# Forty tokens instead of thirty-two on fetched expert rows, the low parts of value units in pairs

## The chip, the cores and the metric

The kernel runs on 1 core of one Trainium2 chip. The time is device microseconds (us) of one execution. The engines are TensorE (PE), VectorE (DVE), ScalarE (ACT), GpSimd (POOL) and SyncE (SP, which only issues transfers here).

## The reference

One layer on 256 tokens of 1024 channels: a mixer (attention and a recurrence), then a feed-forward part that picks, for each token and each of 8 heads, 16 of 16384 experts. An expert is one row of `peer_u` and one row of `peer_v`, 1024 float32 each. The change lies in the feed-forward part.

```python
def peer_ffn(xn, peer_wq, peer_subkeys, peer_u, peer_v):
    q = (xt @ peer_wq).reshape(n_tok, PEER_HEADS, 2, PEER_HALF)        # 256 tokens, 8 heads, 2 x 128
    s = jnp.einsum('thpc,hpnc->thpn', q, peer_subkeys)                 # 128 subkeys for each half
    top_s, top_i = lax.top_k(s, PEER_TOPK)                             # 16 of 128
    cand_s = (top_s[:, :, 0, :, None] + top_s[:, :, 1, None, :])       # 16 x 16 candidates
    cand_i = (top_i[:, :, 0, :, None] * PEER_NKEYS + top_i[:, :, 1, None, :])
    best_s, best_pos = lax.top_k(cand_s, PEER_TOPK)                    # 16 experts of 16384 per head
    idx = jnp.take_along_axis(cand_i, best_pos, axis=-1)
    gates = jax.nn.softmax(best_s, axis=-1)
    def one_chunk(args):
        u_g = peer_u[ic]
        h = jax.nn.gelu(jnp.einsum('chkd,cd->chk', u_g, xc)) * gc      # dot with row of u, gelu, gate
        v_g = peer_v[ic]
        return jnp.einsum('chk,chkd->cd', h, v_g)                      # weighted sum of rows of v

def reference(x, ...):
    xn = rmsnorm(h, norm1_g[l])
    h = h + hybrid_mixer(xn, ...)                                      # attention and a recurrent mixer
    xn = rmsnorm(h, norm2_g[l])
    h = h + peer_ffn(xn, peer_wq[l], peer_subkeys[l], peer_u[l], peer_v[l])
    return rmsnorm(h, normf_g)
```

## The kernel before, in words

**Two ways to compute an expert.** The experts are a grid of 128 x 128. For the first 224 tokens (TD) the kernel computes all 16384 experts densely, in 128 units of 128 experts, and makes the gates of the experts that were not picked zero. For the last 32 tokens (TG) it fetches only the rows that were picked. A token has 8 x 16 = 128 picks. The 128 partitions are 32 tokens times 4 repeats (REPS), so one indirect transfer on GpSimd's queue fetches 128 rows of 4 KB, one for each partition, and 32 of them (GATHERS) cover the u rows, 32 more the v rows. A row that was fetched costs VectorE one operation over 128 x 1024: `dot` (product with the repeated token and sum) for u, `row_added` (sum += coefficient x row) for v.

**A unit.** float32 products are made from high and low parts rounded to TensorE's one-pass type. A u unit (`expert_unit`) is 8 matmuls of the unit's high part with both parts of 224 tokens, 448 columns (L922), and 8 of its low part with the high part of the tokens, 224 columns (L926). A v unit is the same (`wide_value` L988, `low_value` L993). SyncE loads the unit (512 KB) into one of 4 slots (`load`, L396) once the unit four before it is done, ScalarE makes the high part `hi` (L1069), GpSimd the low part `lo` over the raw data (L1509); in the v stage VectorE makes it (L2176).

**The order in the u stage.** 128 units, numbered 0 to 127 here. Beside the first 52, VectorE ranks the picks. From unit 68 (FIRST) the units are gated: after unit n's 16 matmuls, TensorE makes the gates of 4 tokens from one-hot rows with 8 short matmuls (L948, L949; the "hot group"). There are SECOND = 56 of these groups, for 224 tokens, so the last 4 units have none. The hot group of unit n waits for `oh1_low`, which ScalarE makes in `low_one_hots` (L1398) from what VectorE made in `one_hots` (L2092, L2094). ScalarE works strictly in order: in step n it makes `hi` of unit n+2, copies the right half of unit n (L1414), makes gelu of unit n-1 (L1419) and then the low one-hots of unit n+1. VectorE's step n is gates in (L2104), halves (L2111), `gated` of n-1 (L2119) and the one-hots of unit n+2.

**SyncE's queue** is one program in order. After the load of unit 79 it issues 3 transfers that repeat the last 32 tokens over the partitions (L442) and 4 that lay out the picks and gates in the same way (L446), SBUF to SBUF, and then goes on with the load of unit 80.

**GpSimd's queue**: the low parts of all u units; behind each of the last four one fetch; two low parts of v units; then the rest of the fetches, each as soon as one of 4 row buffers is free. VectorE does one `dot` or `row_added` behind every second v unit.

**The end.** The last two v units are interleaved over the 8 output blocks, and one more matmul per block (L1056, float32, two instructions) adds the 32 fetched tokens' sums. Then the output is turned, normalised and stored.

## Time and profile before

| | |
|---|---|
| runs | 987.2, 987.57, 988.05 us, median 987.57 us |
| profiled execution | 987.29 us, its span in the profile 985.5 us |
| granted TensorE clock, mean | 0.998 of full |
| busy | PE 975.0 us (99%), DVE 743.3 (75%), ACT 626.6 (64%), POOL 598.1 (61%) |
| u stage, v stage | from 296 us to 651 us, from 651 us to 977 us |
| transfers | 215.05 MB, mean 218 GB/s; by slice of 24.6 us in the v stage some 315, at most 383 GB/s |

Columns of the views are named where their rows stand. A matmul's own duration overlaps the next ones; how far matmuls are apart is read from the chain of waits, where eight in a row take, for instance, 1.64 us. A time in square brackets is idle time of the engine before the instruction, with what ended it.

### The profile page before, as it was taken

The numbers are of one execution on the slowest core, as the hardware profiler recorded it, in microseconds if no ns is written. First come the engines' busy times: TensorE is split into PE (matmuls) and PEld (weight loads), VectorE is DVE, ScalarE is ACT, GpSimd is POOL, SyncE is SP. The second block draws the span as 40 slices with busy tenths as digits, with TensorE's granted clock in tenths as the row PEclk, the third lists the DMA queues.
The fourth block names the chain that finished last, engine by engine and source line by source line (L and its number), as shares of the span: only waits on it lengthen the run. The fifth ranks groups of instructions, "written<-read, shape, count | busy, mean of one in ns | idle before, by whom it ended". The sixth has DMA issues, their size and how long they took to land.

```text
span 985.5 us, 22607 instructions
## 1 busy us (share of the span) xinstructions
PE 975.0 (99%) x7344; PEld 918.3 (93%) x7344; DVE 743.3 (75%) x1718; ACT 626.6 (64%) x1232; POOL 598.1 (61%) x292
## 2 busy tenths in 40 slices
PE   9999999999999999999999999999999999999997
PEld 8998899999899999999999999989999999999996
DVE  7664663544747797887788888879888878888886
ACT  6774375556556666676988888865555555555553
POOL 3685624687318999989777777874443335444420
PEclk9999999999999999999999999999999999999999
DMA  7463303355545555555554444499888887988871
GB/s 264 141 238 121 128 35 107 129 188 195 204 162 171 210 203 208 211 201 209 188 189 170 170 170 170 171 355 383 311 317 316 317 309 280 333 317 313 305 276 44
DMA packets 61821, 215.05 MB, mean 218 GB/s; under 512 B 7203, under 2 KB 9251, under 8 KB 61644
## 3 DMA queue, kind: packets, MB, share of 16 engines
q1 hardware_dynamic: 51980, 180.04, 51.0%
q0 software_dynamic: 9216, 33.56, 9.4%
q10 hardware_dynamic: 576, 0.82, 0.2%
q8 instruction: 29, 0.48, 0.2%
q14 instruction: 20, 0.16, 0.1%
HBM read 212.89 MB, written 1.06 MB: 217 GB/s over the span
## 4 chain that ended last, share of the span: by engine, by line
PE 96%; POOL 2%; DVE 1%; ACT 1%; DMA 0%; issue 0%; ACTq 0%; DVEq 0%; POOLq 0%
PE PS L988 21%; PE PS L922 21%; PE PS L993 12%; PE PS L926 11%; PE PS L493 4%; PE PS L494 4%; PE PS L495 4%; PE PS L871 3%; PE PS L503 2%; PE PS L879 2%; PE PS L948 1%; POOL lo L1509 1%; PE PS L949 1%; PE PS L657 1%; PE PS L507 1%; PE PS L912 1%
## 5 line engine op out<-in xcount | busy, mean ns | idle before, releaser
L1509 POOL TENSOR_TENSOR lo<-raw,hi 128x1024 fp32r<-128x1024 f32 x191 | 459.4, 2413 | 152.7 <-ACT hi L1069 139.2
L922 PE MATMUL PS<-xb,hi 128*128 128x448 f32 x1024 | 235.0, 371 | 0.0
L1069 ACT CAST hi<-raw 128x1024 fp32r<-128x1024 f32 x203 | 212.7, 1048 | 33.2 <-DMA raw<-in_u_units 12.4
L988 PE MATMUL PS<-xb,hi 128*128 128x448 f32 x1008 | 228.7, 368 | 0.0
L922 PEld LDWEIGHTS PS<-xb,hi 128*128 128x128 f32 x1024 | 183.0, 189 | 12.2
L988 PEld LDWEIGHTS PS<-xb,hi 128*128 128x128 f32 x1008 | 179.9, 189 | 11.8
L2176 DVE TENSOR_TENSOR lo<-raw,hi 128x1024 fp32r<-128x1024 f32 x126 | 154.1, 1223 | 24.2 <-ACT hi L1406 24.1
L1443 ACT CAST xb<-arena 128x224 fp32r (+1 forms) x126 | 47.9, 380 | 143.6 <-PE PS L993 142.3
L926 PEld LDWEIGHTS PS<-xb,lo 128*128 128x128 f32 x1024 | 133.8, 191 | 4.7 <-POOL lo L1509 0.7
L993 PEld LDWEIGHTS PS<-xb,lo 128*128 128x128 f32 x1008 | 132.7, 191 | 4.1
L1406 ACT CAST hi<-raw 128x1024 fp32r<-128x1024 f32 x128 | 133.9, 1046 | 3.4 <-DMA raw<-in_v_units 3.4
L926 PE MATMUL PS<-xb,lo 128*128 128x224 f32 x1024 | 133.9, 273 | 0.4 <-POOL lo L1509 0.4
L993 PE MATMUL PS<-xb,lo 128*128 128x224 f32 x1008 | 132.8, 273 | 0.0
L1549 POOL DMA_INDIRECT arena<-in_v_units,con x32 | 66.5, 2079 | 95.0 <-DVE hot L2170 70.9
L1549 POOL DMA_INDIRECT arena<-in_u_rows,con x32 | 59.5, 1859 | 79.0 <-DVE arena L2163 78.4
L493 PE MATMUL PS<-xb,hi 128*128 128x256 f32 x264 | 76.0, 288 | 0.1
L494 PE MATMUL PS<-xb,hi 128*128 128x256 f32 x264 | 74.7, 283 | 0.0
L495 PE MATMUL PS<-xb,lo 128*128 128x256 f32 x264 | 74.7, 283 | 0.0
L1398 ACT ACTIVATE oh_low<-oh_high,gt 128x128 f16<-128x128 f16 x224 | 70.8, 389 | 0.1
L2157 DVE TENSOR_TENSOR xb<-arena,xb 128x224 fp32r<-128x224 f32 x126 | 52.0, 413 | 18.5 <-ACT xb L1443 18.3
L2092 DVE TENSOR_SCALAR oh_high<-PS,i2T,gT 128x128 f16<-128x128 f16 x224 | 61.2, 336 | 0.1
L2104 DVE SCALAR_TENSOR_TENSOR arena<-PS,arena 128x512 f32 (+1 forms) x56 | 38.8, 692 | 24.5 <-PE PS L949 24.3
(353 smaller groups left out, 1517.0 us busy)
## 6 DMA issues: line engine op xcount, KB each, us to landing
raw<-in_u_units SPq DMA_DIRECT2D x128, 512.0 KB
raw<-in_v_units SPq DMA_DIRECT2D x128, 512.0 KB
raw<-in_w_in_units SPq DMA_DIRECT2D x43, 512.0 KB
raw<-in_w_q_units SPq DMA_DIRECT2D x16, 512.0 KB
raw<-in_w_proj_units SPq DMA_DIRECT2D x8, 512.0 KB
raw<-in_w_out_units SPq DMA_DIRECT2D x8, 512.0 KB
arena<-bias_rows SPq DMA_DIRECT2D x2, 512.0 KB, 5.0
arena<-in_subkeys_t SPq DMA_DIRECT2D x1, 1024.0 KB, 5.4
```

The lines of the kernel that those rows point to most:

```text
L493: mm(ps, hi[:, s, c], mh[:, k, :], start=(k == k0), stop=False)
L494: mm(ps, hi[:, s, c], ml[:, k, :], start=False, stop=False)
L495: last = mm(ps, lo[:, s, c], mh[:, k, :], start=False, stop=(k == k1 - 1))
L922: mm(o[:, 0:2 * TD].rearrange("p (s t) -> p s t", s=2), hi[:, w, P * k:P * k + P], xb[:, k, :, 0:TD], start=(k == 0), stop=False, skip_gro ...
L926: last = mm(o[:, 0:TD], lo[:, w, P * k:P * k + P], xb[:, k, 0, 0:TD], start=False, stop=(k == KT - 1), skip_group_check=True)
L988: return mm(PS[:, V_BANKS[c], 0:2 * TD].rearrange("p (s t) -> p s t", s=2), hi[:, (U_V + j) % 4, P * c:P * c + P], coef_slot(u + j)[:, :, ...
L993: return mm(PS[:, V_BANKS[c], 0:TD], value_slot(j)[:, P * c:P * c + P], coef_slot(u + j)[:, 0, 0:TD], start=False, stop=last, skip_group_c ...
L1069: nc.scalar.copy(hi[:, j, :], raw[:, j, :]).then_inc(hi_made, 1)
L1406: nc.scalar.copy(hi[:, (U_V + j) % 4, :], value_raw(j % 8)).then_inc(hi_made, 1)
L1509: nc.gpsimd.tensor_tensor(lo[:, w, :], raw[:, w, :], hi[:, w, :].bitcast(F32), ALU.subtract).then_inc(lo_pool, 1)
L1549: nc.gpsimd.indirect_dma_start(out=rows_at[g % 4], out_offset=None, in_=rows, in_offset=bass.IndirectOffsetOnAxis(ap=pick_row[:, n:n + 1], ...
L2176: V.tensor_tensor(value_slot(j), value_raw(j), hi[:, (U_V + j) % 4, :].bitcast(F32), ALU.subtract).then_inc(lo_dve, 1)
```

## The change

Tokens on fetched rows go from 32 to 40, as two groups: 32 tokens x 4 repeats as before, and the last 8 tokens x 16 repeats, with 8 fetches of u rows and 8 of v rows. TD is 216, so the dense matmuls have 432 and 216 columns. SECOND is 54, so 6 units at the end of the u stage have no hot group. In all there are 80 fetches and 80 row operations.

- SyncE repeats the 8 tokens with 15 more transfers and lays out their picks with 16 more, all at the same place in its queue.
- GpSimd fetches the first 8 (the u rows of the second group) behind the low parts of units 84, 88, ... 112, and VectorE makes their dots in the gated steps of units 88, 92, ... 116, ahead of the one-hots of that step. The loops there are written out.
- The other 72 row operations are spread evenly over the v stage, in the order of the list ROW_WORK.
- VectorE makes `gl` and `lo` of value units two at a time: one operation over 2 x 216 and one over 2 x 1024 columns.
- ScalarE copies the repeated rows of both groups (4 copies for 2) and makes gelu of the first dots apart.
- One more matmul per output block adds the second group.

```diff
-TG = 32
+GROUPS = [32, 8]
+TG = sum(GROUPS)
 TD = T - TG
 SECOND = TD // 4
-FIRST = NKEYS - SECOND - 4
+FIRST = 68
 GATED_UNITS = NKEYS - FIRST
-REPS = P // TG
-GATHERS = P // REPS
+REPEATS = [P // tokens for tokens in GROUPS]
+GATHERS = sum(GROUPS)
+COLUMNS = [slice(0, GROUPS[0]), slice(GROUPS[0], GATHERS)]
+PICKS_IN = 16 * (2 * sum(REPEATS) - 2)
 PICKS_AT = 13
...
-        row_sums = hot[:].rearrange("p a b c d -> p (a b c d)")[:, D:2 * D]
+        repeated = [xrep[:], area(P * TD + 4 * D, D)]
+        row_sums = [hot[:].rearrange("p a b c d -> p (a b c d)")[:, D:2 * D], repeated[1]]
...
+        def value_pair(q, parts, more):
+
+            if q == 0:
+                return parts[:, 3::-3, :]
+            return parts[:, 1:3, :] if q == 1 else more[q - 2]
...
-            sp.wait_ge(xrep_sb, 2)
-            for q in range(1, REPS):
-                sp.dma_start(xrep[TG * q:TG * q + TG, :], xrep[0:TG, :]).then_inc(picks_in, 16)
+            sp.wait_ge(xrep_sb, 4)
+            for rows, n, times in zip(repeated, GROUPS, REPEATS):
+                for q in range(1, times):
+                    sp.dma_start(rows[n * q:n * q + n], rows[0:n]).then_inc(picks_in, 16)
             sp.wait_ge(staged_made, 2)
             sp.wait_ge(picks_ps, 3)
-            for q in range(REPS):
-                sp.dma_start(picks[TG * q:TG * q + TG], staged[P - TG:P, :, GATHERS * q:GATHERS * q + GATHERS]
-                             ).then_inc(picks_in, 16)
+            for n, times, columns_of, at in zip(GROUPS, REPEATS, COLUMNS, (P - TG, P - GROUPS[1])):
+                for q in range(times):
+                    sp.dma_start(picks[n * q:n * q + n, :, columns_of], staged[at:at + n, :, n * q:n * q + n]
+                                 ).then_inc(picks_in, 16)
             with sp.Fori(20, 32) as i:
...
-            with pe.Fori(FIRST // 4 + 1, NKEYS // 4 - 1) as i:
+            with pe.Fori(FIRST // 4 + 1, NKEYS // 4 - 2) as i:
                 for j in range(4):
                     pe.wait_ge(coef_made, 4 * i + (j - FIRST - 3 + 2))
                     gated_unit(i, j)
+            for j in range(4):
+                pe.wait_ge(coef_made, GATED_UNITS - 8 + j - 3 + 2)
+                if GATED_UNITS - 8 + j < SECOND:
+                    gated_unit(NKEYS // 4 - 2, j)
+                else:
+                    expert_unit(NKEYS // 4 - 2, j)
             for j in range(4):
...
-                mm(PS[:, V_BANKS[c], 2 * TD:2 * TD + TG], row_sums[:, P * c:P * c + P], taker, start=False, stop=True,
-                   skip_group_check=True).then_inc(acc_done, 1)
+                for n, columns_of in enumerate(COLUMNS):
+                    last = mm(PS[:, V_BANKS[c], 2 * TD + columns_of.start:2 * TD + columns_of.stop],
+                              row_sums[n][:, P * c:P * c + P], takers[n], start=False, stop=True, skip_group_check=True)
+                last.then_inc(acc_done, 1)
...
+            act.wait_ge(rows_used, GROUPS[1])
+            nc.scalar.activation(pick_dot[:, early_dots], pick_dot[:, early_dots], ACT.Gelu).then_inc(dots_gelu, 1)
...
-            with pool.Fori(0, NKEYS // 4 - 1) as i:
+            with pool.Fori(0, GATHER_AT) as i:
                 for j in range(4):
                     make_lo(U_U, i, j)
-            pool.wait_ge(picks_in, 16 * (2 * REPS - 1))
+            pool.wait_ge(picks_in, PICKS_IN)
+            for g in range(GROUPS[1]):
+                make_lo(U_U, GATHER_AT + g, 0)
+                if g >= 4:
+                    pool.wait_ge(rows_used, g - 3)
+                gather(g)
+                for j in range(1, 4):
+                    make_lo(U_U, GATHER_AT + g, j)
+            with pool.Fori(GATHER_AT + GROUPS[1], NKEYS // 4 - 1) as i:
+                for j in range(4):
+                    make_lo(U_U, i, j)
             for j in range(4):
                 make_lo(U_U, NKEYS // 4 - 1, j)
-                gather(j)
+                pool.wait_ge(rows_used, GROUPS[1] + j - 3)
+                gather(GROUPS[1] + j)
             make_lo(U_V, 0, 0)
             make_lo(U_V, 0, 1)
-            for g in range(4, 2 * GATHERS):
+            for g in range(GROUPS[1] + 4, 2 * GATHERS):
                 pool.wait_ge(rows_used, g - 3)
                 gather(g)
...
+            def dot(g):
+
+                group = 0 if g >= GROUPS[1] else 1
+                n = ROW_WORK[g][1]
+                dve.wait_ge(rows_in[g % 4], 16 * (g // 4) + 16)
+                V.scalar_tensor_tensor(out=rows_at[g % 4], in0=rows_at[g % 4], scalar=1.0, in1=repeated[group], op0=ALU.mult,
+                                       op1=ALU.mult, accum_out=pick_dot[:, n:n + 1]).then_inc(rows_used, 1)
+
+            def gated_step(i, j, early_dot=None):
+
+                gates_in(i, j)
+                second_halves(i, j)
+                gated(i, j - 1, 4)
+                if early_dot is not None:
+                    dot(early_dot)
+                one_hots(i, j + 2)
+
+            first_dots = GATHER_AT + 1 - FIRST // 4
+            final = GATED_UNITS // 4 - 1
+            with dve.Fori(1, first_dots) as i:
                 for j in range(4):
-                    gates_in(i, j)
-                    second_halves(i, j)
-                    gated(i, j - 1, 4)
-                    one_hots(i, j + 2)
-            final = SECOND // 4
+                    gated_step(i, j)
+            dve.wait_ge(picks_in, PICKS_IN)
+            for g in range(GROUPS[1]):
+                for j in range(4):
+                    gated_step(first_dots + g, j, g if j == 0 else None)
+            for i in range(first_dots + GROUPS[1], final - 1):
+                for j in range(4):
+                    gated_step(i, j)
...
-            def value_operands(i, j):
-                make_gl(2 * i + j // 4, j % 4)
-                dve.wait_ge(hi_made, 8 * i + (U_V + j + 1))
-                V.tensor_tensor(value_slot(j), value_raw(j), hi[:, (U_V + j) % 4, :].bitcast(F32), ALU.subtract).then_inc(lo_dve, 1)
+            def make_gl_pair(i, j):
+                dve.wait_ge(gh_made, 4 * i + (j + 2))
+                V.tensor_tensor(xb[:, j:j + 2, 1, 0:TD], coef[:, bass.ds(4 * i + j, 2), :], xb[:, j:j + 2, 0, 0:TD].bitcast(F32),
+                                ALU.subtract).then_inc(gl_made, 2)
+
+            def row_added(g):
+
+                n = ROW_WORK[g][1]
+                sums = row_sums[0 if n < GROUPS[0] else 1]
+                dve.wait_ge(rows_in[g % 4], 16 * (g // 4) + 16)
+                if n in (0, GROUPS[0]):
+                    V.tensor_scalar(sums, rows_at[g % 4], pick_coef[:, n:n + 1], None, ALU.mult).then_inc(rows_used, 1)
+                    return
+                dve.wait_ge(rows_used, g)
+                V.scalar_tensor_tensor(out=sums, in0=rows_at[g % 4], scalar=pick_coef[:, n:n + 1], in1=sums, op0=ALU.mult,
+                                       op1=ALU.add).then_inc(rows_used, 1)
+
+            def pick_coefs(n):
+
+                dve.wait_ge(dots_gelu, 2 - n)
+                part = COLUMNS[n]
+                link(V.tensor_tensor(pick_coef[:, part], pick_dot[:, part], pick_gate[:, part], ALU.mult))
+
+            def value_operands(i, q):
+                make_gl_pair(2 * i + q // 2, q % 2 * 2)
+                dve.wait_ge(hi_made, 8 * i + (U_V + 2 * q + 2))
+                V.tensor_tensor(value_pair(q, lo, lo_pairs), value_pair(q, raw, raw_pairs), value_pair(q % 2, hi, None).bitcast(F32),
+                                ALU.subtract).then_inc(lo_dve, 2)
...
+            g = GROUPS[1]
+            pick_coefs(1)
+            for q in range(1, NKEYS // 2):
+                value_operands(q // 4, q % 4)
+                while g < min(2 * GATHERS, ROWS_AFTER[q]):
+                    if ROW_WORK[g][0]:
+                        dot(g)
+                    else:
+                        if ROW_WORK[g] == (False, 0):
+                            pick_coefs(0)
+                        row_added(g)
+                    g += 1
 
...
+GATHER_AT = 21
+ROW_WORK = [(True, GROUPS[0] + n) for n in range(GROUPS[1])]
+for n in range(GROUPS[0]):
+    ROW_WORK.append((True, n))
+    if n % 6 == 5:
+        ROW_WORK.append((False, GROUPS[0] + n // 6))
+ROW_WORK += [(False, GROUPS[0] + n) for n in range(5, 8)] + [(False, n) for n in range(GROUPS[0])]
+ROWS_AFTER = [GROUPS[1] + len(ROW_WORK[GROUPS[1]:]) * q // (NKEYS // 2 - 3) for q in range(NKEYS // 2)]
+LAST_DOT = ROW_WORK.index((True, GROUPS[0] - 1))
+DOTS_DONE = next(q for q in range(NKEYS // 2) if ROWS_AFTER[q] > LAST_DOT) // 4
```

SyncE's queue around the load of unit 80, before:

```order
L436 REGISTER_ALU
L436 COMPARE_AND_BRANCH
L442 DMA xrep<-xrep 32x1024 [waits repeated_rows_sb]
L442 DMA xrep<-xrep 32x1024 x2
L446 DMA con<-arena 32x2x32 [waits picks_ps,gathered_picks_staged]
L446 DMA con<-arena 32x2x32 x3
L448 UNCONDITIONAL_BRANCH
L448 ISA
L396 ISA [waits unit_multiplied]
L396 DMA raw<-in_u_units 128x1024
```

The same place now (the two rows at L457 end the loop whose last load is unit 79, and the last row is the load of unit 80):

```order
L457 REGISTER_ALU
L457 COMPARE_AND_BRANCH
L464 DMA xrep<-xrep 32x1024 [waits repeated_rows_sb]
L464 DMA xrep<-xrep 32x1024 x2
L464 DMA arena<-arena 8x1024 x15
L469 DMA con<-arena 32x2x32 [waits picks_ps,gathered_picks_staged]
L469 DMA con<-arena 32x2x32 x3
L469 DMA con<-arena 8x2x8 x16
L471 UNCONDITIONAL_BRANCH
L471 ISA
L417 ISA [waits unit_multiplied]
L417 DMA raw<-in_u_units 128x1024
```

Thirty-one transfers have come in between the two loads: 38 stand there for 7.

VectorE's queue in a gated step, before (L2104 the gates, L2119 the products of the unit before, L2092 and L2094 the one-hots):

```order
L2104 SCALAR_TENSOR_TENSOR arena<-PS,arena 128x128x4 [waits coef_made,gates_made]
L2111 TENSOR_TENSOR PS<-PS,con 128x224 [waits right_half_of_expert_unit_copied]
L2119 TENSOR_TENSOR arena<-PS,arena 128x224 [waits gates_used,act_evacuated]
L2092 TENSOR_SCALAR oh_high<-PS,i2T,gT 128x128 [waits gates_made]
L2092 TENSOR_SCALAR oh_high<-PS,i2T,gT 128x128 x3
L2094 TENSOR_TENSOR oh_52<-PS,i_half 128x512
```

The same step now where it has a dot (L2195 is the dot):

```order
L2154 SCALAR_TENSOR_TENSOR arena<-PS,arena 128x128x4 [waits coef_made,gates_made]
L2161 TENSOR_TENSOR PS<-PS,con 128x216 [waits right_half_of_expert_unit_copied]
L2169 TENSOR_TENSOR arena<-PS,arena 128x216 [waits gates_used,act_evacuated]
L2195 SCALAR_TENSOR_TENSOR arena,con<-arena 128x1024 [waits gathered_rows_in2]
L2142 TENSOR_SCALAR oh_high<-PS,i2T,gT 128x128 [waits gates_made]
L2142 TENSOR_SCALAR oh_high<-PS,i2T,gT 128x128 x3
L2144 TENSOR_TENSOR oh_52<-PS,i_half 128x512
```

The dot stands between the products of the unit before and the one-hots of the unit two ahead.

## Rows read from the trace of the kernel before

**Rows 1.** Page, chain that ended last, share of the span by engine.

```profile
PE 96%; POOL 2%; DVE 1%; ACT 1%; DMA 0%; issue 0%; ACTq 0%; DVEq 0%; POOLq 0%
```

**Rows 2.** Chain of waits (start us, us, what), before the u stage: 512, 256, 128 columns.

```profile
269.27 1.84 PE PS L871 x8
271.11 0.95 PE PS L879 x8
...
288.82 7.15 PE PS L912 x64
```

**Rows 3.** Chain of waits, one v unit: 448 and 224 columns.

```profile
959.81 1.64 PE PS L988 x8
961.44 0.88 PE PS L993 x8
```

**Rows 4.** Timeline of SyncE's queue (start us, us, engine, line, operation, out<-in), 493 to 500 us.

```profile
493.94 1.89 SPq L442 DMA_DIRECT2D xrep<-xrep  x3
495.94 2.86 SPq L446 DMA_DIRECT2D con<-arena  x4
...
498.20 0.60 SPq L446 DMA_DIRECT2D con<-arena  x1
499.16 0.34 SPq L396 DMA_DIRECT2D raw<-in_u_units  x1
```

**Rows 5.** Timeline of SyncE's queue, a transfer of 8 partitions by itself.

```profile
31.20 0.34 SPq L416 DMA_DIRECT2D bias_rows<-arena  x1
```

**Rows 6.** Timeline, ScalarE after that load, and TensorE's hot group of unit 79.

```profile
502.32 1.05 ACT L1069 CAST hi<-raw 128x1024 fp32r<-128x1024 f32 x1 [1.19 <-DMA raw<-in_u_units]
...
503.78 1.26 ACT L1398 ACTIVATE oh_low<-oh_high,gt 128x128 f16<-128x128 f16 x4
...
505.25 0.25 PE L948 MATMUL PS<-oh_high,oh 128*128 128x128 f16 x1
```

**Rows 7.** Timeline of GpSimd, VectorE, ScalarE and TensorE, one gated step.

```profile
630.15 2.41 POOL L1509 TENSOR_TENSOR lo<-raw,hi 128x1024 fp32r<-128x1024 f32 x1 [0.65 <-ACT hi L1069]
...
631.78 0.38 DVE L2119 TENSOR_TENSOR arena<-PS,arena 128x224 f32<-128x224 f32 x1
...
633.09 0.42 DVE L2094 TENSOR_TENSOR oh<-PS,i_half 128x512 f16<-128x512 f16 x1
...
633.96 1.26 ACT L1398 ACTIVATE oh_low<-oh_high,gt 128x128 f16<-128x128 f16 x4
...
636.30 0.25 PE L948 MATMUL PS<-oh_high,oh 128*128 128x128 f16 x1
```

**Rows 8.** Groups by line, 640 to 970 us: count | busy us, mean ns | idle before.

```profile
L2176 DVE TENSOR_TENSOR lo<-raw,hi 128x1024 fp32r<-128x1024 f32 x126 | 154.1, 1223 | 24.2 <-ACT hi L1406 24.1
...
L2170 DVE SCALAR_TENSOR_TENSOR hot<-arena,con,hot 128x1024 f32<-128x1024 f32 x31 | 39.7, 1281 | 0.0
L2163 DVE SCALAR_TENSOR_TENSOR arena<-arena,xrep 128x1024 f32<-128x1024 f32 x32 | 39.0, 1219 | 0.0
```

**Rows 9.** Timeline of GpSimd and VectorE where the v stage begins.

```profile
650.67 4.73 POOL L1509 TENSOR_TENSOR lo<-raw,hi 128x1024 fp32r<-128x1024 f32 x2
...
652.39 3.28 DVE L2157 TENSOR_TENSOR xb<-arena,xb 128x224 fp32r<-128x224 f32 x1
```

**Rows 10.** Windows (us, then busy of PE, PEld, DVE, ACT, POOL, clock, DMA, GB/s), the end.

```profile
980.00:983.00 3.00, 0.00 (x0) 0.00 (x0) 1.78 (x4) 1.79 (x5) 0.00 (x0) 0.92 0.39 147
983.00:985.50 2.50, 0.00 (x0) 0.00 (x0) 0.00 (x0) 0.00 (x0) 0.00 (x0) 0.50 0.66 243
```

**Rows 11.** Timeline of TensorE, its first 16 matmuls.

```profile
1.34 3.76 PE L535 MATMUL PS<-warm 128*128 128x224 f32 x16 [1.34 <-DVE i1T L1607]
```

**Rows 12.** Timeline of ScalarE, high part of the fourth v unit.

```profile
656.09 1.05 ACT L1406 CAST hi<-raw 128x1024 fp32r<-128x1024 f32 x1 [1.16 <-DMA raw<-in_v_units]
```

**Rows 13.** Chain of waits: low pass of the third v unit; one block's added matmul.

```profile
658.64 0.88 PE PS L993 x8
...
975.16 0.15 PE PS L1056 x2
```

More of the change, by code:

```diff
@@ L119, in block_program, with two_pairs @@
         ident_r = nc.alloc_sbuf_tensor_at("ident_r", [P, P], F32R, offset=con_at + 4 * C_CEN)
-        taker = con[:, C_BLK:C_BLK + TG]
-        picks = con[:, C_BLK + TG:C_BLK + TG + 2 * GATHERS].rearrange("p (a b) -> p a b", a=2)
+        takers = [con[:, C_BLK:C_BLK + GROUPS[0]], con[:, C_CEN + 2 * GATHERS:C_CEN + 2 * GATHERS + GROUPS[1]]]
+        picks = con[:, C_BLK + GROUPS[0]:C_BLK + GROUPS[0] + 2 * GATHERS].rearrange("p (a b) -> p a b", a=2)
         pick_row, pick_gate = picks[:, 0, :].bitcast(U32), picks[:, 1, :]
-        pick_dot = con[:, C_BLK + TG + 2 * GATHERS:C_IOTA]
         pick_coef = con[:, C_CEN:C_CEN + GATHERS]
+        pick_dot = con[:, C_CEN + GATHERS:C_CEN + 2 * GATHERS]
         more_at = [xb_at + 4 * 8 * T, xb_at + 4 * 12 * T, early_at, con_at + 4 * C_M4]
-        more_raw = [nc.alloc_sbuf_tensor_at(f"raw{RAW + j}", [P, D], F32, offset=at) for j, at in enumerate(more_at)]
-        more_lo = [nc.alloc_sbuf_tensor_at(f"lo{RAW + j}", [P, D], F32R, offset=at) for j, at in enumerate(more_at)]
+        apart = (more_at[2] - more_at[3]) // 4
+        def two_pairs(kind, dt):
+            near = nc.alloc_sbuf_tensor_at(f"{kind}4_5", [P, 2, D], dt, offset=more_at[0])
+            far = nc.alloc_sbuf_tensor_at(f"{kind}7_6", [P, 2, apart], dt, offset=more_at[3])
+            return near[:], far[:, ::-1, 0:D]
+        raw_pairs, lo_pairs = two_pairs("raw", F32), two_pairs("lo", F32R)
         rms = small[:, 56:60]
@@ L376, in value_slot, with value_pair @@
         def value_slot(j):
-            return lo[:, (U_V + j) % 4, :] if j < RAW else more_lo[j - RAW][:]
+            return lo[:, (U_V + j) % 4, :] if j < RAW else lo_pairs[j // 2 - 2][:, j % 2, :]
         def value_raw(j):
-            return raw[:, (U_V + j) % 4, :] if j < RAW else more_raw[j - RAW][:]
+            return raw[:, (U_V + j) % 4, :] if j < RAW else raw_pairs[j // 2 - 2][:, j % 2, :]
+        def value_pair(q, parts, more):
+            if q == 0:
+                return parts[:, 3::-3, :]
+            return parts[:, 1:3, :] if q == 1 else more[q - 2]
+        def value_pair(q, parts, more):
+            if q == 0:
+                return parts[:, 3::-3, :]
+            return parts[:, 1:3, :] if q == 1 else more[q - 2]
         def value_landing(j):
@@ L1365, in _ @@
                 act.wait_ge(xrep_ps, b + 1)
-                nc.scalar.copy(xrep[0:TG, 512 * b:512 * b + 512], PS[0:TG, 2 + b, :]).then_inc(xrep_sb, 1)
+                for rows, columns_of in zip(repeated, COLUMNS):
+                    nc.scalar.copy(rows[0:columns_of.stop - columns_of.start, 512 * b:512 * b + 512],
+                                   PS[columns_of, 2 + b, :]).then_inc(xrep_sb, 1)
             with act.Fori(1, PICKS_AT) as i:
@@ L1427, in _ @@
                 low_one_hots(0, j + 1)
-            with act.Fori(1, SECOND // 4 - 1) as i:
+            final = GATED_UNITS // 4 - 1
+            with act.Fori(1, final - 1) as i:
                 for j in range(4):
@@ L1451, in _ @@
             for j in range(4):
-                second_right_copy(SECOND // 4, j, last=True)
-                second_half_gelu(SECOND // 4, j - 1)
+                second_right_copy(final, j, last=True)
+                second_half_gelu(final, j - 1)
                 if j == 1:
@@ L1464, in _ @@
                 value_ahead(0, j)
-            with act.Fori(1, GATHERS // 4) as i:
+            with act.Fori(1, DOTS_DONE) as i:
                 for j in range(8):
@@ L1546, in gather @@
             def gather(g):
-                rows, n = (u_rows if g < GATHERS else v_t.rearrange("n p d -> (n p) d")), g % GATHERS
+                dots, n = ROW_WORK[g]
+                rows = u_rows if dots else v_t.rearrange("n p d -> (n p) d")
                 nc.gpsimd.indirect_dma_start(
@@ L2147, in _ @@
+            for g in range(GROUPS[1]):
[4 more added lines that the diff above has]
+                    gated_step(i, j)
             for j in range(4):
-                gates_in(final - 1, j)
+                n = 4 * final - 4 + j
+                if n < SECOND:
+                    gates_in(final - 1, j)
                 second_halves(final - 1, j)
-                gated(final - 1, j - 1, 4)
@@ L2178, in _ @@
             for j in range(4):
                 second_halves(final, j)
-                gated(final, j - 1, 3 - j)
+                gated(final, j - 1, SECOND + 3 - 4 * final - j)
                 if j == 1:
@@ L2185, in _ @@
                                         ALU.subtract).then_inc(gl_made, 1)
[L2186 removed]
+            gated(final, 3, SECOND - 4 * final - 1)
             dve.wait_ge(coef_made, GATED_UNITS + 2)
[L2188 to L2224 removed]
+            g = GROUPS[1]
[10 more added lines that the diff above has]
+                    g += 1
             for c in range(KT):
```

92 lines of the change are left out of this document (21 added, 71 removed).

## The prediction

> **What bounds the kernel now.** I read the chain of waits by engine first: TensorE is 96% of it [rows 1]. So two things count: how long its units take, and where it would begin to wait. Next the chain in order of time, which gives the distance between matmuls by shape; then the timelines of the other queues at the places that the change touches, to see how late each may be.
>
> Eight matmuls of 512 columns take 1.84 us, eight of 448 take 1.64 [rows 2, 3], so 64 columns less are 25 ns a matmul, 0.39 ns a column (2.4 GHz would be 0.42). The low passes behave otherwise: eight of 256 columns take 0.95 us (119 ns each), eight of 224 take 0.88 (110 ns), and 64 float32 instructions of 128 columns take 7.15 us, 112 ns each [rows 2, 3]. From 224 down to 128 nothing is gained: there is a floor at 110 to 112 ns.
>
> **Columns.** A unit loses 16 columns in each of 8 high matmuls: 8 x 16 x 0.39 ns = 50 ns. Its low matmuls stand on the floor already: 0 ns, with a bound of 18 ns from the slope between 256 and 224 (9 ns over 32 columns, x 8 columns x 8). Of 256 units some 6 lie where GpSimd sets the pace (the four fetches behind the last low parts), where TensorE only waits longer. 250 x 50 ns = -12.5 us, bound 250 x 68 ns = -17.
>
> The Trainium skill has this floor ("TensorE: Matmul & The Clock Gate", LDWEIGHTS): a weight load takes its columns over 1.2 GHz, estimated 107 ns for 128 float32 columns. The same page's gap for a matmul by itself, columns over 2.4 GHz plus 2.5 ns, would let the low pass shrink as well. By the first the columns bring what I count, by the second about 7 us more; the rows at 128 and 224 columns side with the first.
>
> **Hot groups.** Those of units 79 and 122 start at 505.25 and 636.30 [rows 6, 7], 43 units in 131.05 us, 3.05 a unit against 2.52 without one. Two go: -1.05 us. Behind them GpSimd's low parts and fetches are the limit; ScalarE has no low one-hots there and is earlier by their 1.26 us, so part of it stays. I take -0.7 (0 to -1.05).
>
> **SyncE's queue.** This is the large term. Before, 7 small transfers stand between the loads of units 79 and 80. Three took from 493.94 to 495.94, 0.67 us each, four from 495.94 to 498.80, 0.72 each; the load of unit 80 follows at 499.16 [rows 4]. Now 38 stand there: 31 more. What is queued behind: the load of unit 80, 3.2 us later its high part on ScalarE (502.32, which waited 1.19 us for that load), then, since ScalarE goes in order, the copy of unit 78, a gelu, and the low one-hots of unit 79, done at 503.78 + 1.26 = 505.04. TensorE wanted them at 505.25 [rows 6]. So the slack at unit 79's hot group was 0.2 us, and its four shorter units (76 to 79) use it up. Every microsecond that the load is later is one that TensorE stands still: stall = 31 x t.
>
> t is not in the trace for 8 partitions, SBUF to SBUF. From above: 0.72, the transfers that lay out picks. From below: a transfer of 8 partitions to memory by itself took 0.34 [rows 5], with some 0.04 between two: 0.38. The nearest by kind are the seven SBUF to SBUF ones, the last of them 0.60 [rows 4]; smaller ones should not cost more. I take 0.55: 17.0 us (11.8 to 22.3). What would hide it is only a load issued ahead, and there is none: slot and queue are both in order. Nothing later gives it back, since TensorE is the bound again at once.
>
> **The clock.** After the last matmul, near 979, the granted clock is 0.92 of full in 980 to 983 and 0.50 in the stretch after it [rows 10]: it fell to the low of its two levels (1.2 GHz) with TensorE idle for some microseconds. A stall of 11 us and more ends there. Coming back costs what the start shows: 16 matmuls of 224 columns in 3.76 us [rows 11] where 110 ns each is 1.76 [rows 3]. +2.0 us (0 to 3).
>
> **Eight dots in gated steps.** VectorE reaches the place of the dot at 631.78 + 0.38 = 632.16. GpSimd then works on a low part until 632.56 [rows 7]. The dot reads two SBUF operands, and the trace has such an operation starved: 224 columns from SBUF took 3.28 us, from 652.39 to 655.67, until GpSimd's two low parts, 650.67 to 655.40, were through [rows 9]. So the dot waits 0.40, runs 1.22 [rows 8] and 0.08 for its sum: 1.70 us late. Queued behind it are the one-hots of the unit two ahead, ready at 633.51 and used by ScalarE at 633.96, done 635.22, wanted by TensorE at 636.30 [rows 7]: slack 0.45 + 1.08 = 1.53. Late by 0.17, with units shorter by 0.05 (two in between) 0.3, and VectorE's spare 0.4 a step over four steps only just makes up 1.70. I take 0.4 each: +3.2 us. Bounds: 0 (no waiting for GpSimd, 1.3 < 1.53) and a whole low part of 2.41, 2.0 more each: +19. The eight fetches cost GpSimd about 1 us each; its low parts are ready 2.85 us before use (632.56 against 636.30 - 0.88), which hides them. If that cover were gone: 8 x 1.
>
> The Trainium skill calls this pair of ports an exclusive lock ("SBUF — State Buffer", two separate sides): whoever starts first holds it for its whole instruction. The 3.28 us agree. It is the rule that speaks most against this place; with it the price depends on where in GpSimd's 2.4 us VectorE arrives.
>
> **Value units in pairs.** One operation of 2048 for two of 1.22 us saves their fixed part, and the row operations (1.28 and 1.30 with its sum [rows 8]) go from one to 72/61 = 1.18 a pair. VectorE: about 2.3 + 0.6 + 1.5 = 4.4 us of 4.94. It stays under TensorE and saves nothing there. What it costs is at the start: the low part of the third v unit now waits for the high part of the fourth, made at 656.09 + 1.05 = 657.14 [rows 12]; a pair of 2.3 us ends at 659.5, and TensorE wants it at 658.64 [rows 13]. +1.0 us (0 to 2). Later pairs have 2.8 us of slack.
>
> **The end.** One more float32 matmul per block, two instructions, 0.15 us as the one that is there [rows 13] to twice the floor, 0.22: 8 x 0.18 = +1.4 us, on the chain.
>
> **Nothing:** two more copies on ScalarE early in the u stage (about 1 us, in a queue with spare time), the second small reduction, the second gelu. 16 more fetches of 0.5 MB are 8 MB over 316 us, 26 GB/s beside some 315 in the v stage, whose busiest slice had 383 with TensorE not waiting.
>
> **Sum:** -12.5 - 0.7 + 17.0 + 2.0 + 3.2 + 1.0 + 1.4 = +11.4 us. The profiled execution took 987.3 (span 985.5), 0.3 under the median of the runs: 998.7, I say 999.
>
> **Rivals.**
> - *The burst is cheap.* If 31 small transfers cost under 0.2 us each, the stall is under 6 us. The rest is -13.2 + 5.6 = -7.6, or -5.6 with the clock, so it decides at t = 0.18: above, slower; at t near 0 the time is 980. For it: transfers that small are nowhere in that queue back to back. Against it: no transfer in rows 4 and 5 costs under 0.33.
> - *The dots wait for whole low parts.* After the first, ScalarE and GpSimd are late too, and VectorE may arrive just as GpSimd starts: +16 more, 1015. Against: arriving later brings it nearer to the end of the same low part.
> - *The dots are free*: 3.2 less, 995.5. For it: VectorE catches up within the step.
> - *The low pass shrinks too*: 8 columns at 2.4 GHz are 3.3 ns x 2048 matmuls = 6.8 us, 992. Against: 110 ns at 224 and 112 at 128.
>
> **How the numbers follow.** The forecast 0.52, with its own range 992 to 1006 from t and the dots; cheap burst 0.10; whole low parts 0.10; free dots 0.14; low pass 0.14. About 0.2% (2 us) is what a measurement of this kernel tells from no change. Faster holds most of the cheap burst and the tail of the low pass at t = 0.38: 0.10. Same: 0.05. Slower: 0.85. Range 988 to 1010: it leaves out the cheap burst and most of the whole low parts.
>
> **What would show it.** Right: SyncE's queue has 38 small transfers in a row, some 20 us, with ScalarE's high part of unit 80 waiting that long for its load, TensorE idle about 17 us near 500 us and a granted clock below full in that one slice; v units 2.47 us apart, low passes still 0.88. Wrong: a load of unit 80 within 12 us of the first small transfer, TensorE waiting for one-hots by over 1 us at each dot, or low passes of 0.86 and less.

## The result: slower by 3.0%, where 1.2% was forecast

The changed kernel takes 1017.51 us (median of 4 runs, 1016.93 to 1018.56) against 987.81 for the kernel before (4 runs, 987.2 to 988.64): a ratio of 1.0301, interval 1.0283 to 1.0319. That is +29.7 us where +11.4 was forecast, and outside the range of 988 to 1010. The profiled executions have spans of 1016.8 and 985.5 us, with a mean granted clock of 0.978 and 0.998. One of the four runs of *e1* below took 1158.59 us at a mean granted clock of 0.752 and is left out of *e1*'s numbers.

Where the time went is read from the starts of TensorE's high passes, unit by unit, in both traces. The second column is how much later (+) or earlier (-) the changed kernel is at that point, the third what came in since the row above:

| at the high pass of | after minus before, us | in between | |
|---|---|---|---|
| first u unit | +0.2 | | |
| u unit 79 | -5.5 | -5.7 | columns |
| u unit 81 | +19.7 | +25.2 | SyncE's queue and the clock |
| u unit 120 | +35.1 | +15.4 | dots, less 3.1 for columns |
| third v unit | +34.1 | -1.0 | columns and two hot groups |
| sixth v unit | +38.5 | +4.4 | start of the v stage |
| third last v unit | +29.7 | -8.8 | columns |
| end of the span | +31.3 | +1.6 | end |

### The profile page after: what moved, and what is told of

It reads as the page before. It is cut to its first block, busy times and chain, and to the rows that moved or that the text cites. A ratio compares the mean times of both kernels' runs of the same rounds, so it can differ in the third digit from the quotient of the medians.

```text
span 1016.8 us, 21865 instructions
## 1 busy us (share of the span) xinstructions
PE 968.4 (95%) x7344; PEld 927.2 (91%) x7344; DVE 758.3 (75%) x1606; ACT 623.2 (61%) x1227; POOL 572.0 (56%) x308
## 4 chain that ended last, share of the span: by engine, by line
PE 74%; issue 11%; POOL 11%; DVE 2%; DMA 1%; ACT 1%; POOLq 0%; ACTq 0%; SPq 0%; DVEq 0%
PE PS L1017 19%; PE PS L1022 11%; POOL lo L1546 10%; PE PS L945 10%; PE PS L949 6%; PE PS L516 4%; PE PS L517 4%; PE PS L518 4%; PE PS L526 2%; PE PS L971 1%; PE PS L972 1%; PE PS L894 1%; PE PS L680 1%; PE PS L530 1%; DMA raw<-in_v_units 1%
## 5 line engine op out<-in xcount | busy, mean ns | idle before, releaser
L945 PE MATMUL PS<-xb,hi 128*128 128x432 f32 x1024 | 229.8, 367 | 0.0
L1017 PE MATMUL PS<-xb,hi 128*128 128x432 f32 x1008 | 220.4, 360 | 0.0
L945 PEld LDWEIGHTS PS<-xb,hi 128*128 128x128 f32 x1024 | 186.5, 192 | 5.6
L1017 PEld LDWEIGHTS PS<-xb,hi 128*128 128x128 f32 x1008 | 180.4, 190 | 5.6
L2254 DVE TENSOR_TENSOR lo<-raw,hi 128x2048 fp32r<-128x2048 f32 x63 | 144.4, 2292 | 19.8 <-ACT hi L1439 11.9
L949 PEld LDWEIGHTS PS<-xb,lo 128*128 128x128 f32 x1024 | 136.2, 194 | 3.4 <-POOL lo L1546 1.8
L1022 PEld LDWEIGHTS PS<-xb,lo 128*128 128x128 f32 x1008 | 133.3, 192 | 4.7 <-DVE lo L2254 3.1
L949 PE MATMUL PS<-xb,lo 128*128 128x216 f32 x1024 | 136.3, 276 | 0.9 <-POOL lo L1546 0.8
L1022 PE MATMUL PS<-xb,lo 128*128 128x216 f32 x1008 | 133.5, 274 | 2.7 <-DVE lo L2254 2.7
L1480 ACT CAST xb<-arena 128x216 fp32r (+1 forms) x126 | 47.0, 373 | 138.7 <-PE PS L1022 138.7
L1587 POOL DMA_INDIRECT arena<-in_v_units,con x40 | 51.3, 1283 | 117.0 <-DVE hot L2242 74.9
L1587 POOL DMA_INDIRECT arena<-in_u_rows,con x40 | 49.8, 1244 | 82.3 <-DVE arena L2195 77.7
L971 PE MATMUL PS<-oh_high,oh 128*128 128x128 f16 x216 | 32.6, 231 | 34.5 <-issue 34.4
L971 PEld LDWEIGHTS PS<-oh_high,oh 128*128 128x128 f16 x216 | 23.6, 116 | 37.0 <-issue 36.1
```

The lines of the kernel that those rows point to most:

```text
L945: mm(o[:, 0:2 * TD].rearrange("p (s t) -> p s t", s=2), hi[:, w, P * k:P * k + P], xb[:, k, :, 0:TD], start=(k == 0), stop=False, skip_gro ...
L949: last = mm(o[:, 0:TD], lo[:, w, P * k:P * k + P], xb[:, k, 0, 0:TD], start=False, stop=(k == KT - 1), skip_group_check=True)
L1017: return mm(PS[:, V_BANKS[c], 0:2 * TD].rearrange("p (s t) -> p s t", s=2), hi[:, (U_V + j) % 4, P * c:P * c + P], coef_slot(u + j)[:, :, ...
L1022: return mm(PS[:, V_BANKS[c], 0:TD], value_slot(j)[:, P * c:P * c + P], coef_slot(u + j)[:, 0, 0:TD], start=False, stop=last, skip_group_c ...
L1587: nc.gpsimd.indirect_dma_start(out=rows_at[g % 4], out_offset=None, in_=rows, in_offset=bass.IndirectOffsetOnAxis(ap=pick_row[:, n:n + 1], ...
L2254: V.tensor_tensor(value_pair(q, lo, lo_pairs), value_pair(q, raw, raw_pairs), value_pair(q % 2, hi, None).bitcast(F32), ALU.subtract).then ...
```

## The profile after

From the page of the changed kernel: TensorE's busy share and its granted clock by slice, and below them the chain by engine, the same view as [rows 1]:

```profile
PE   9999999999999999999649888998999999999997
PEclk9999999999999999999969899999999999999999
...
PE 74%; issue 11%; POOL 11%; DVE 2%; DMA 1%; ACT 1%; POOLq 0%; ACTq 0%; SPq 0%; DVEq 0%
```

A slice is 25.4 us. TensorE has a hole in slices 20 and 21 (from 483 to 534 us), shallow ones in slices 23 to 25 and one more in slice 28 (686 to 712 us); behind that it is as full as before. That GpSimd is 11% of the chain is no bottleneck by itself: 11% is 112 us, and TensorE, busy for 968.4 of 1016.8 us, was idle for less than half of that. The chain follows low parts back through stretches in which TensorE works.

The chain of waits, one v unit, the same view as [rows 3] (start us, us, what):

```profile
761.88 1.56 PE PS L1017 x8
763.45 0.89 PE PS L1022 x8
...
1002.28 0.36 PE PS L1086 x4
```

The high pass went from 1.64 to 1.565 us (1.56 and 1.57 in turn), the low one stayed at 0.88. The last row is to be compared with the end of [rows 13]: a block's added matmuls are four instructions now, 0.36 us for 0.15.

The timeline of SyncE's queue, to be compared with [rows 4] (start us, us, engine, line, operation, out<-in, count):

```profile
488.65 1.91 SPq L464 DMA_DIRECT2D xrep<-xrep  x3
490.60 10.58 SPq L464 DMA_DIRECT2D arena<-arena  x15
501.30 14.34 SPq L469 DMA_DIRECT2D con<-arena  x20
516.00 2.14 SPq L417 DMA_DIRECT2D raw<-in_u_units  x4
```

From the first small transfer to the next load are 27.35 us; before they were 5.22. The 31 more took 22.1 us, 0.71 each. What TensorE did meanwhile, from the chain of waits:

```profile
498.92 0.88 PE PS L949 x8
499.80 22.58 issue
522.38 0.27 PE PS L971
...
523.40 2.99 PE PS L945 x8
526.39 1.67 PE PS L949 x8
...
528.66 1.60 PE PS L945 x8
530.26 0.88 PE PS L949 x8
```

One idle stretch of 22.6 us (the chain calls it "issue", since no releaser shows in the profile; TensorE did nothing in it), then eight short matmuls and one unit at the low level of the clock: 2.99 us for 1.60 and 1.67 for 0.88. The windows (us, then busy of PE, PEld, DVE, ACT, POOL, clock, DMA, GB/s) have the granted clock:

```profile
498.00:500.00 2.00, 1.80 (x13) 1.59 (x11) 0.16 (x1) 0.00 (x0) 0.00 (x0) 1.00 0.44 53
500.00:522.00 22.00, 0.00 (x0) 0.00 (x0) 1.11 (x4) 2.43 (x7) 1.30 (x1) 0.60 0.26 76
522.00:529.00 7.00, 6.62 (x35) 6.34 (x36) 3.70 (x13) 4.73 (x13) 5.82 (x3) 0.56 0.20 81
```

Full before the stall, 0.60 on the mean of it, 0.56 in the 7 us behind it: TensorE worked at 1.2 GHz there, for 0.56 is near half, and came back to 2.4 by 528.66.

The eight dots, as a group of VectorE between 535 and 680 us:

```profile
L2195 DVE SCALAR_TENSOR_TENSOR arena<-arena 128x1024 f32<-128x1024 f32 x8 | 22.7, 2842 | 0.0
```

2.84 us on the mean, where the same operation takes 1.22 by itself [rows 8]. The mean hides two kinds: three of the eight, the second, fourth and sixth, took 4.85 to 4.88, the others 1.5 to 1.8. One of the three, on the timelines of GpSimd, VectorE and ScalarE, the views of [rows 7] and [rows 9]:

```profile
561.58 0.96 POOL L1587 DMA_INDIRECT arena<-in_u_rows,con  x1
562.56 7.10 POOL L1546 TENSOR_TENSOR lo<-raw,hi 128x1024 fp32r<-128x1024 f32 x3
...
565.88 4.88 DVE L2195 SCALAR_TENSOR_TENSOR arena<-arena 128x1024 f32<-128x1024 f32 x1
...
572.24 1.28 ACT L1431 ACTIVATE oh_low<-oh_high,gt 128x128 f16<-128x128 f16 x4 [4.48 <-DVE oh L2144]
```

GpSimd's three low parts ran back to back from 562.56 to 569.66. The dot was issued at 565.88 into the second of them and ended at 570.76, 1.1 us (its own time) behind the third. The one-hots stand behind it, ScalarE waited 4.48 us for those, and TensorE for ScalarE. The first dot, a short one, by GpSimd's timeline and VectorE's:

```profile
549.36 4.81 POOL L1546 TENSOR_TENSOR lo<-raw,hi 128x1024 fp32r<-128x1024 f32 x2
555.67 2.39 POOL L1546 TENSOR_TENSOR lo<-raw,hi 128x1024 fp32r<-128x1024 f32 x1 [1.50 <-ACT hi L1100]
```

```profile
553.67 1.57 DVE L2195 SCALAR_TENSOR_TENSOR arena<-arena 128x1024 f32<-128x1024 f32 x1
```

It was issued in the second of two low parts, which ended at 554.17, and ended 1.1 us behind that one. Behind that low part GpSimd had to wait for its next high part. So it is in all eight: the dot got in where GpSimd paused, and where GpSimd's next low part was ready, GpSimd went on first. The windows show that at the long dots too the clock went:

```profile
566.00:574.00 8.00, 4.49 (x38) 4.27 (x37) 8.00 (x14) 3.26 (x8) 3.66 (x2) 0.91 0.58 197
574.00:580.00 6.00, 6.00 (x32) 5.69 (x31) 3.32 (x12) 3.73 (x11) 5.30 (x3) 0.55 0.19 46
```

TensorE was idle for some 3.5 us, and from 574 on the next unit ran at 0.55. By the distances between units, each of the three cost 4.9 to 6.3 us, the other five 0.3 to 0.6.

The start of the v stage, chain of waits, and the rows of ScalarE and VectorE in it. They are to be compared with [rows 9], [rows 12] and [rows 13]:

```profile
684.82 7.10 DMA raw<-in_v_units
...
691.94 1.06 ACT hi L1439
...
693.09 2.30 DVE lo L2254
...
695.44 2.04 PE PS L1022 x8
697.47 2.28 PE PS L1017 x8
```

The fourth value load landed 7.1 us after its issue, the pair's low part waited for it, and TensorE for the pair, with the clock low again behind that.

## Experiments

All are the changed kernel with one thing different, but for *e5* and *e6*, which start from the kernel before. The kernel before took 987.89 us beside *e1* to *e4* and 988.06 beside *e5* to *e8*.

### e1_spread: the small transfers spread over the loads

```
             with sp.Fori(0, 10) as i:        # was (0, 20)
...
             for u in range(40, 80):
                 sp.wait_ge(unit_done, U_U + u - 3)
                 load(u_t[u], (U_U + u) % 4)
...
                 small = copies[u - 40:u - 39] if u < 60 else layouts[u - 60:u - 59]
                 for dst, src in small:
                     sp.dma_start(dst, src).then_inc(picks_in, 16)
```

> The changed kernel with the 38 small transfers of SyncE's queue issued one behind each of the loads of units 40 to 79, no two in a row. Theory: the 31 added ones hold back the load of unit 80, and the stall of 22.6 us there with its low-clock tail (2.7 us) goes: 1017.5 - 25 = 992 us, plus or minus 2. Rival: the small transfers cost somewhere else too (landing, DMA engines), and spreading them only moves the stall: over 1005 us.

Measured: 993.21 us (median of three runs, 992.95 to 993.77), ratio 1.0052 (1.0032 to 1.0072), 24.3 less than the changed kernel. Timeline of SyncE's queue, one small transfer and the next load:

```profile
480.19 0.71 SPq L476 DMA_DIRECT2D con<-arena  x1
482.79 0.32 SPq L417 DMA_DIRECT2D raw<-in_u_units  x1
```

In the trace TensorE goes from unit 79 to 81 without a stall (-4.8 and -5.0 against the kernel before, where the changed kernel has -5.5 and +19.7). A single transfer takes its 0.5 to 0.9 us of the queue as a rule, but the queue waits for TensorE there anyway (a unit is 2.45 to 2.97 us). By unit 79 this kernel is 0.7 us behind the changed one: that is the most that the 38 transfers cost when each has a load behind it, against 24 us when they stand in a row.

### e2_turns: GpSimd lets the dot go first

GpSimd makes the last low part of a group of four, which is the one that a dot's wait runs into longest, only when the dot has read its row.

```
                 for j in range(1, 4):
+                    if j == 3 and g:
+                        pool.wait_ge(rows_used, g)
                     make_lo(U_U, GATHER_AT + g, j)
```

(The loop over the eight groups is shifted accordingly by one more.)

> The changed kernel with one more wait on GpSimd: after the low part that runs when a dot comes up, it waits for that dot before it starts the next low part. Theory: three of the eight dots (4.88 us for 1.22) starve because GpSimd, behind by its fetch, runs three low parts back to back and never frees the shared port; with a gap made for each dot it waits for one low part at most, the large stalls (about 5.5 us each with the clock) shrink to some 0.5 each: -14 to -16 us, 1002 us. Rival: the dots are late because their rows land late, or the wait costs GpSimd more than it gives: 1015 us or more.

Measured: 1006.48 us, ratio 1.019 (1.0173 to 1.0207), 11.0 less than the changed kernel. The dots took 2.32 us on the mean. The second of them, by the timelines of GpSimd and of VectorE:

```profile
562.14 4.74 POOL L1546 TENSOR_TENSOR lo<-raw,hi 128x1024 fp32r<-128x1024 f32 x2
568.06 2.38 POOL L1546 TENSOR_TENSOR lo<-raw,hi 128x1024 fp32r<-128x1024 f32 x1 [1.18 <-DVE arena L2198]
```

```profile
565.46 2.51 DVE L2198 SCALAR_TENSOR_TENSOR arena<-arena 128x1024 f32<-128x1024 f32 x1
```

Two low parts in a row now, until 566.88, and the dot ends 1.1 us behind them. The long waits are gone (no more 4.88), but six of the eight dots still cost TensorE 1.28 each (units of 4.25 us for 2.97), the first and the last 0.4 and 0.6. From unit 90 to 120 the kernel falls 6.4 us behind the one before, the changed one 16.1. More than expected is left (8.7 us for some 4), since nearly every dot now comes up early in a low part and waits 1.4 us for the rest of it; in the changed kernel five of the eight waited 0.3 to 0.6.

### e3_psum_dots: the dots' second operand in PSUM

```
+                if group:
+                    V.scalar_tensor_tensor(out=..., in0=..., scalar=1.0,
+                                           in1=PS[:, 7, :].unsqueeze(1).to_broadcast([P, 2, 512]), ...
+                    return
                 V.scalar_tensor_tensor(out=rows_at[g % 4], in0=rows_at[g % 4], scalar=1.0, in1=repeated[group], ...
```

Place, length and GpSimd's work are the same; the dots of the last 8 tokens multiply by whatever is in PSUM, so that part isn't computed.

> The changed kernel with the second operand of the eight early dots read from a PSUM bank instead of the repeated tokens in SBUF (the dots of the last 8 tokens are then not computed); same place, same size, same fetches. Theory of the shared port: one SBUF operand needs no turn, each dot takes 1.3 us, none 4.9: 1.3 is under the slack of 1.53, so -18 us, 999 us. Rival (the dots' own 1.3 us on a VectorE without spare time, or late rows, are the cost): within 3 us of 1017.5.

Measured: 996.82 us, ratio 1.0093 (1.0076 to 1.011), 20.7 less: 18.5 between units 81 and 120, and 2.7 at the start of the v stage. GpSimd's row and VectorE's at the same place as above:

```profile
561.50 7.10 POOL L1546 TENSOR_TENSOR lo<-raw,hi 128x1024 fp32r<-128x1024 f32 x3
```

```profile
564.83 1.21 DVE L2196 SCALAR_TENSOR_TENSOR arena<-arena,PS 128x1024 f32<-128x1024 f32 x1
```

GpSimd again runs three low parts back to back, until 568.60, and the dot is done in 1.21 us in the middle of them. All eight took 1.21. So it isn't VectorE's queue, nor the fetched row, that was late in the changed kernel: with two operands in SBUF the dot waits for GpSimd, with one it doesn't.

The Trainium skill says why ("SBUF — State Buffer", two separate sides): VectorE with two SBUF inputs and GpSimd need one pair of ports, which is locked for a whole instruction. The 1.21 and the 4.88 us agree with it; that GpSimd goes on to its next instruction while VectorE stands waiting is what these rows add.

### e4_single: the third and fourth v unit singly

```
+            for j in (2, 3):
+                dve.wait_ge(gh_made, j + 1)
+                V.tensor_tensor(xb[:, j, 1, 0:TD], coef[:, j, :], xb[:, j, 0, 0:TD].bitcast(F32), ALU.subtract)...
+                dve.wait_ge(hi_made, U_V + j + 1)
+                V.tensor_tensor(value_slot(j), value_raw(j), hi[:, (U_V + j) % 4, :].bitcast(F32), ...
             for q in range(1, NKEYS // 2):
-                value_operands(q // 4, q % 4)
+                if q > 1:
+                    value_operands(q // 4, q % 4)
```

> The changed kernel with the operands of value units 2 and 3 made singly as before, all later ones in pairs. Theory: 4.4 us at the start of the v stage are the third unit's low part waiting for the fourth unit's load, which lands 7.1 us after its issue: -3.5 to -4.5 us, 1013.5 us. Rival: the fourth unit needs the same load itself soon after, so that most of the wait only moves one unit on: -1 us or less.

Measured: 1015.7 us, ratio 1.0276 (1.0259 to 1.0293), 1.8 less. The trace shows the term itself gone: the third and fourth v unit are 2.45 us apart, where the changed kernel has 6.35, and from the last u unit to the sixth v unit the loss is 0.4 instead of 4.8. Its profile keeps 3.0 of that (span 1013.7), for it is 1.4 behind the changed kernel's before it comes there, in part by a longer unit 68 (3.81 us for 3.13); its median keeps 1.8. So the place and its 4.4 us are shown, and what the whole kernel gets from it is less than expected.

### e5_before_31: 31 small transfers added to the kernel before

```
+            for q in range(15):
+                sp.dma_start(rows_at[0][8 * q + 8:8 * q + 16], xrep[0:8]).then_inc(picks_in, 16)
...
+            for q in range(16):
+                sp.dma_start(rows_at[1][8 * q:8 * q + 8, 0:16]..., staged[P - 8:P, :, 8 * q:8 * q + 8])...
```

The waits for these transfers count 31 more.

> The kernel before the change with 31 more small transfers at the place of its 7 (15 copies of 8 rows of 4 KB and 16 of 8 rows of 2 x 8 numbers, SBUF to SBUF, to free space), nothing else of the change. Theory: they cost what they cost in the changed kernel, 31 x 0.71 = 22 us less the slack, and the low clock 2.5: 987.9 + 24 = 1012 us. Rival: in the changed kernel the stall came from something else that its 216 columns or fetches brought: under 1000 us.

Measured: 1012.21 us, ratio 1.0239 (1.0223 to 1.0255), +24.2. Timeline of SyncE's queue:

```profile
494.00 1.90 SPq L442 DMA_DIRECT2D xrep<-xrep  x3
495.94 10.36 SPq L444 DMA_DIRECT2D arena<-xrep  x15
506.42 2.64 SPq L448 DMA_DIRECT2D con<-arena  x4
509.10 11.66 SPq L451 DMA_DIRECT2D arena<-arena  x16
521.12 2.14 SPq L396 DMA_DIRECT2D raw<-in_u_units  x4
```

The chain of waits of the same kernel:

```profile
505.47 22.20 issue
527.66 0.27 PE PS L952
```

Fifteen from 495.94 to 506.42 are 0.70 us each, sixteen from 509.10 to 521.12 are 0.75. The load of unit 80 is issued at 521.12 where it was 499.16 [rows 4], and TensorE is idle for 22.2 us. From unit 81 to the end the distance to the kernel before is 25.1 us in the profile and stays so: nothing gives it back. This term alone costs twice what the whole change was forecast to.

### e6_sizes: other widths

From the kernel before: low passes of the u stage on 128 columns (224 before), high passes of the v stage on 400 (448), that part of the products left out.

```
-    last = mm(o[:, 0:TD], lo[:, w, P * k:P * k + P], xb[:, k, 0, 0:TD], start=False,
+    last = mm(o[:, 0:128], lo[:, w, P * k:P * k + P], xb[:, k, 0, 0:128], start=False,
...
```

> The kernel before with fewer columns in two places (that part of the products is left out): low passes of the u stage on 128 columns for 224, high passes of the v stage on 400 for 448. If the low pass stands on a floor, u units stay 2.52 us apart (rival: columns at 2.4 GHz, 8 x 96 = 0.32 us less, 2.20). The high pass: at 0.42 ns a column 48 x 8 = 0.16 us less, at the 0.55 that the changed kernel showed from 448 to 432, 0.21 us less; if the gain comes in steps, something else.

Chain of waits, a u unit and a v unit:

```profile
405.45 1.68 PE PS L922 x8
407.13 0.84 PE PS L926 x8
...
763.95 0.88 PE PS L993 x8
764.84 1.46 PE PS L988 x8
```

The low pass of 128 columns has 0.84 us in its row where those of 224 and 216 have 0.88, but the high pass beside it has 1.68 where it had 1.64, and the u units stay 2.52 us apart, as expected: the floor of 110 ns a matmul stands down to 128 columns. In the v stage the high pass takes 1.64, 1.565 and 1.455 us at 448, 432 and 400 columns. That is 0.59 ns a column for the first 16 and 0.43 for the next 32; between 512 and 448 it was 0.39 [rows 2, 3]. The kernel ran in 962.01 us (one run).

### e7_dots_last: the dot behind the one-hots

The dot stands behind the one-hots of its step instead of ahead of them, with GpSimd's wait of *e2* kept.

```
-                if early_dot is not None:
-                    dot(early_dot)
                 one_hots(i, j + 2)
+                if early_dot is not None:
+                    dot(early_dot)
```

> The changed kernel with GpSimd waiting for each early dot before its next low part, and the dot behind the one-hots of its step instead of ahead of them. Theory: then the one-hots are on time, the dot comes when the low part in front of it ends, and what it delays (the next step's gates by 0.9 us) has 1.5 us of slack: the eight dots cost under 0.3 us each, -16 to -18 us, 1000.5 us. Rival: GpSimd's low parts, 1.6 us later at each dot, or the gates become the wait: 1004 us or more (with the dots ahead of the one-hots it was 1006.5).

Measured: 996.44 us, ratio 1.0091 (1.0072 to 1.011), 21.1 less than the changed kernel and 10.0 less than *e2*. The group of the eight dots, 535 to 680 us:

```profile
L2198 DVE SCALAR_TENSOR_TENSOR arena<-arena 128x1024 f32<-128x1024 f32 x8 | 9.8, 1220 | 0.0
```

1.22 us each with both operands in SBUF, and from unit 81 to 120 the kernel gains 3.1 us on the one before, which is just the columns: the dots cost nothing. Behind the one-hots VectorE arrives when GpSimd has already stopped to wait for it. Also, from the last u unit to the sixth v unit it falls behind by 1.9 us where the changed kernel does by 4.8: 2.9 us of the start of the v stage went together with the dots' stalls, which is why more was gained than the 16 to 18 us expected.

### e8_all: spread, dots last, and the two v units singly

The edits of *e1*, *e7* and *e4* together; everything is computed.

> The changed kernel with all three: small transfers spread over the loads, the dots last with GpSimd's wait, value units 2 and 3 singly. If the three losses are apart: 1017.5 - 24.0 - 17 - 3 = 973.5 us, which beats the kernel before by 14. If one of them hides another (the dots behind the stall, or the fourth value load), up to 980.

Measured: 972.13 us (median of 5, 969.95 to 972.99), ratio 0.9832 (0.9818 to 0.9846): 15.9 less than the kernel before, 45.4 less than the changed one, and close to the 973.5 expected. The three edits took off 24.3, 21.1 and 1.8 each by itself, so the losses stand apart. The page's row of the slices and the chain:

```profile
PE   9999999999999999999999999999999999999997
PEclk9999999999999999999999999999999999999999
...
PE 75%; POOL 13%; issue 7%; DVE 2%; DMA 1%; ACT 1%; POOLq 0%; ACTq 0%; DVEq 0%
```

No hole before the last slice and no slice below full clock. At units 79, 81, 120, the sixth v unit and the third last the trace is at -4.9, -5.1, -8.3, -9.4 and -18.2 against the kernel before: a nearly straight line with the columns' slope.

## Why the prediction was off

The sign and the largest cause were right, the sum was too small by 18 us. Step by step:

| term | forecast | measured | shown by |
|---|---|---|---|
| columns, with hot groups | -13.2 | -18.6 | trace, unit distances |
| SyncE's queue, TensorE idle | +17.0 | +22.6 | *e1*, *e5* |
| clock behind it | +2.0 | +2.6 | trace; *e5* |
| eight dots | +3.2 | +18.5 | *e3*, *e7* |
| start of the v stage | +1.0 | +4.4 | *e4*, *e7* in part |
| end | +1.4 | +1.6 | trace |
| sum | +11.4 | +31.1 | |

**The step that failed is the eight dots.** They were put at 3.2 us, 0.4 each, and cost 18.5; with 3.2 in its place the measured terms would add up to 15.8, inside the range. The step read where GpSimd stands when VectorE arrives from a gated step of before: one low part, over at 632.56 [rows 7]. But the change puts a fetch in front of it, and its cost was booked apart ("ready 2.85 us before use, which hides them"). It does hide them from TensorE, and the lateness stays with GpSimd: behind the fetch its next high parts are ready already, so it can run three low parts with no gap. (That the fetch brings this about is read from these rows; no run took the fetch alone away.) A dot that falls in the second waits for the third as well. [Rows 9] had this in them, 3.28 us over two low parts, and I took only the remainder of one. The rival of whole low parts had the right mechanism, with one low part each, 16 more; it got 0.10. What happened is fewer and dearer: three times the rest of one low part and the whole of the next, and a low clock behind each. *e3* takes the shared operand away and leaves GpSimd's rows as they were, *e7* takes the meeting away: both give the 18.5 back.

**SyncE's queue: mechanism right, t was mis-sized.** 0.71 us for 0.55, at the top end of its range. The bound from above, 0.72, was nearly the rate itself. "Smaller ones should not cost more" did not hold: 8 partitions of 16 columns took 0.75 in *e5*, 8 of 1024 columns 0.70, where the seven larger ones of before took 0.67 and 0.72. The pull down came from the transfer of [rows 5], which stands by itself. What a transfer costs by itself was no bound for a row of them. Of the 22.6 us that TensorE was idle, 22.1 are 31 x t; where the other 0.5 comes from was not pulled apart.

**Columns: better than the bound.** A unit is shorter by 0.073 to 0.08 us in both stages, where 0.050 was worked out and 0.068 was the end. The floor was right, low passes stayed at 0.88. The slope from 512 to 448 does not hold from 448 to 432: the high pass alone gave 0.075. *e6* has 0.43 ns a column below 432, so the step at 448 is dearer than on either side. Why is open.

**Start of the v stage.** The pair was seen, but with its load on time as before (1.16 us behind in [rows 12]). It landed 7.1 us after issue. In *e7* the same pair cost 1.9 in place of 4.8 from there, and in *e1*, with the long dots but without the burst, 3.3: so part of it hangs on where the earlier stalls leave the loads. Without the pair the same stretch cost 0.4, with the stalls (*e4*) and without them (*e8*). So the pair is what waits, in the changed kernel for the fourth load; why the wait is longer behind the stalls was not shown.

**The clock.** Its cost behind the long stall was about right, 2.6 us for 2.0: eight short matmuls and one unit at the low level. That stalls of some 3.5 us also end at the low level was not in the forecast, since the dots were taken to cost 0.4; it is part of their 18.5.

## What to carry to other kernels

A queue that goes in order charges a row of small transfers to whatever load is behind it: count them times the rate of the nearest row of such transfers, or put one behind each load, where 38 of them cost under 1 us here. When VectorE and GpSimd both read two operands from SBUF, ask not how long GpSimd's present instruction lasts but how many it has ready, and what the same change put in front of it; move VectorE's operation behind what others wait for, or let it read one operand from PSUM. A change whose gain (18.6 us here) is hidden under two stalls is worth taking apart, for the stalls can go and the gain stay.
